# Second FFN of a decoder step: which engine forms the sums of weights and their low parts

## The reference

```python
def swiglu(x, w_gate, w_up, w_down):
    return (jax.nn.silu(x @ w_gate) * (x @ w_up)) @ w_down

h = h + 0.5 * swiglu(rmsnorm(h, ffn2_norm), ffn2_w_gate, ffn2_w_up, ffn2_w_down)   # D=1024, D_FF=2816
```

## Time and profile before

| | |
|---|---|
| three runs | 1963.45, 1974.09, 1972.76 us; median 1972.76 |
| the profiled execution | 1961.99 us |
| its span, first to last instruction | 1960.2 us, granted clock 0.985 |
| TensorE matmul busy | 1888.5 us, 96% |
| VectorE busy | 1115.8 us, 57% |
| ScalarE busy | 504.4 us, 26% |
| GpSimd busy | 536.9 us, 27% |

### The profile page before, as it was taken

How to read it: one execution, slowest core, us unless ns; L and a number is a source line. 1 busy time by engine, 2 the same in 40 slices (tenths; PEclk the granted TensorE clock), 3 DMA queues, 4 the chain that set the end, 5 groups by cost and what they waited for, 6 DMA issues and landing times.

```text
span 1960.2 us, 31184 instructions
## 1 busy us (share of the span) xinstructions
PE 1888.5 (96%) x12097; PEld 1865.1 (95%) x12097; DVE 1115.8 (57%) x1962; ACT 504.4 (26%) x927; POOL 536.9 (27%) x606
## 2 busy tenths in 40 slices
PE   7999999999999999999999997999999999999998
PEld 6999999999999999899999987899999999999997
DVE  6556455554545556613775588655565556455646
ACT  5331211111121112432111435322222223222223
POOL 3388200000000000401995035322332223222320
PEclk8999999999999999899999997999999999999999
DMA  4122211112121211046113610111111111111112
GB/s 149 42 65 82 64 32 44 53 32 64 32 64 32 63 33 44 22 100 113 41 44 71 150 43 28 43 55 44 54 44 55 43 55 44 55 44 55 44 47 90
DMA packets 152061, 111.56 MB, mean 57 GB/s; under 512 B 7267, under 2 KB 144035, under 8 KB 151829
## 3 DMA queue, kind: packets, MB, share of 16 engines
q1 hardware_dynamic: 151220, 106.95, 19.3%
q0 software_dynamic: 736, 3.19, 0.6%
HBM read 97.03 MB, written 13.09 MB: 56 GB/s over the span
## 4 chain that ended last, share of the span: by engine, by line
PE 47%; DVE 8%; issue 1%; ACT 1%; DVEq 0%; ACTq 0%
PE bank_pair L780 10%; PE bank_pair L782 9%; PE bank_pair L781 9%; PE bank_down L780 5%; PE bank_down L782 5%; PE bank_down L781 5%; DVE HT L1653 2%; DVE T L1930 1%; DVE HL L2050 1%; DVE HL L1644 1%; DVE HR L2018 1%; PE bank_pair L870 0%; PE bank_down L926 0%; DVE WL L1639 0%; PE bank_pair L1028 0%
## 5 line engine op out<-in xcount | busy, mean ns | idle before, releaser
L780 PE MATMUL bank_pair<-XH,WH 128*128 128x344 f32 x1440 | 466.7, 324 | 14.9 <-POOL XL L2176 5.2
L781 PE MATMUL bank_pair<-XL,WH 128*128 128x344 f32 x1440 | 462.2, 321 | 0.0
L782 PE MATMUL bank_pair<-XH,WL 128*128 128x344 f32 x1440 | 462.1, 321 | 0.0
L1655 DVE SCALAR_TENSOR_TENSOR HT<-bank_down,HT 128x344 f32<-128x344 f32 x518 | 267.0, 516 | 324.4 <-PE bank_down L782 324.2
L780 PEld LDWEIGHTS bank_pair<-XH,WH 128*128 128x128 f32 x1440 | 272.7, 189 | 21.1 <-POOL XL L2176 8.9
L781 PEld LDWEIGHTS bank_pair<-XL,WH 128*128 128x128 f32 x1440 | 272.6, 189 | 0.0
L782 PEld LDWEIGHTS bank_pair<-XH,WL 128*128 128x128 f32 x1440 | 272.6, 189 | 0.0
L2008 DVE SCALAR_TENSOR_TENSOR HT<-bank_down,HT 128x344 f32<-128x344 f32 x264 | 134.7, 514 | 217.1 <-PE bank_down L782 217.1
L780 PE MATMUL bank_pair<-XHM,U_hi 128*128 128x344 f32 x704 | 227.6, 323 | 15.1 <-DVE HR L2018 12.8
L782 PE MATMUL bank_pair<-XHM,U_lo 128*128 128x344 f32 x704 | 226.1, 321 | 0.0
L781 PE MATMUL bank_pair<-XLM,U_hi 128*128 128x344 f32 x704 | 225.8, 321 | 0.0
(11 more groups left out here) (279 smaller groups left out, 3341.4 us busy)
## 6 DMA issues: line engine op xcount, KB each, us to landing
RAW<-in_ffn_w_gate SPq DMA_DIRECT2D x22, 512.0 KB, 5.9
RAW<-in_ffn_w_up SPq DMA_DIRECT2D x22, 512.0 KB, 6.8
RAW<-in_ffn_w_down SPq DMA_DIRECT2D x22, 512.0 KB, 3.5
RAW<-in_w_in SPq DMA_DIRECT2D x16, 512.0 KB, 4.1
DQ_raw<-in_ffn_w_down SPq DMA_DIRECT2D x29, 256.0 KB, 2.9
U_raw<-in_ffn_w_gate SPq DMA_DIRECT2D x22, 256.0 KB, 2.9
AST<-in_ffn_w_gate SPq DMA_DIRECT2D x22, 256.0 KB, 3.0
AST<-in_ffn_w_up SPq DMA_DIRECT2D x22, 256.0 KB, 2.8
```

What stands on the lines that cost most here:

```text
L780: pe.matmul(out, wh, xh, start=first, stop=False)
L781: pe.matmul(out, wh, xl, start=False, stop=False)
L782: return pe.matmul(out, wl, xh, start=False, stop=last)
L1655: ins = dve.scalar_tensor_tensor(ht, tile, scale, ht, ALU.mult, ALU.add)
```

## The change

GpSimd's loop over the passes from the second on is removed; in the first pass it works as before. VectorE forms S1, S2, S3 in the branch V2a and S4 in M3, and computes the low parts of all units: S1 and A11 in M3, S3, A21, S2, A12 in M4, S4 in V2b, and A22 in the branch V1b of the next pass. In odd passes the low parts of a quarter and of the second block of h move from the branch M5 behind the three sums in V2a. The orders of TensorE, ScalarE and SP stay as they are.

```diff
-                dve.tensor_tensor(UL[k][:, :], UR[k][:, :], f(UH[k][:, :]), ALU.subtract).then_inc(unit_ready[k], 1)
+                raw = AST[k - 2] if k in (A21, A22) else UR[k]
+                dve.tensor_tensor(UL[k][:, :], raw[:, :], f(UH[k][:, :]), ALU.subtract).then_inc(unit_ready[k], 1)
...
+            def make(t, k):
+
+                dve.wait_ge(products, unit_used(t - 1, k))
+                if k == S1:
+                    dve.wait_ge(a_in[A21], 16 * (t + 1))
+                    dve.wait_ge(a_in[A22], 16 * (t + 1))
+                    ins = dve.tensor_tensor(UR[S1][:, :], AST[0][:, :], AST[1][:, :], ALU.add)
...
+                ins.then_inc(s_made, 1)
...
+                        if name == "V1b" and t > 0:
+                            unit_lo(t, A22)
                         if name == "V2a":
+                            make(t + 1, S1)
+                            make(t + 1, S2)
+                            make(t + 1, S3)
+                        if name == "M3":
+                            c12(t)
                             unit_lo(t + 1, S1)
                             unit_lo(t + 1, A11)
-                        if name == "M3":
-                            c12(t)
-                            unit_lo(t + 1, S3)
                             quarter_lo(4 * p)
+                            make(t + 1, S4)
                         if name == "M4":
                             c21(t)
+                            unit_lo(t + 1, S3)
+                            unit_lo(t + 1, A21)
                             unit_lo(t + 1, S2)
                             unit_lo(t + 1, A12)
                         if name == "V2b":
+                            unit_lo(t + 1, S4)
                             quarter_lo(4 * p + 1)
                     else:
                         if name == "V1b":
                             mul(t, "V1b", "v", (0, 0))
+                            unit_lo(t, A22)
...
-                        if name == "M5":
-                            quarter_lo(4 * p + 2)
-                            h_lo2(p, 1)
                         if name == "M7":
                             u3_c22_u4(t)
                             mul_sum(t, "C22", (1, 2))
                         if name == "V2a":
                             if more:
-                                unit_lo(t + 1, S1)
-                                unit_lo(t + 1, A11)
+                                make(t + 1, S1)
+                                make(t + 1, S2)
+                                make(t + 1, S3)
+                            quarter_lo(4 * p + 2)
+                            h_lo2(p, 1)
                             h_lo2(p, 2)
                         if name == "M3":
                             c12(t)
                             mul_sum(t, "C12", (0, 2))
                             if more:
-                                unit_lo(t + 1, S3)
+                                unit_lo(t + 1, S1)
+                                unit_lo(t + 1, A11)
+                                make(t + 1, S4)
                         if name == "M4":
                             c21(t)
                             mul_sum(t, "C21", (1, 1))
                             h_lo2(p, 3)
                             if more:
+                                unit_lo(t + 1, S3)
+                                unit_lo(t + 1, A21)
+                                unit_lo(t + 1, S2)
                                 unit_lo(t + 1, A12)
                         if name == "V2b":
                             mul(t, "V2b", "y", (1, 0))
                             h_lo2(p, 4)
                             if more:
-                                unit_lo(t + 1, S2)
+                                unit_lo(t + 1, S4)
                             h_lo2(p, 5)
...
-            for t in range(1, PASSES):
-                make(t, S1)
-                make(t, S2)
-                make(t, S3)
-                unit_lo(t, A21)
-                make(t, S4)
-                unit_lo(t, A22)
-                unit_lo(t, S4)
```

More of the change, by code:

```diff
@@ L1996, in unit_lo @@
                 dve.wait_ge(u_hi, hi_count(t, k))
-                dve.tensor_tensor(UL[k][:, :], UR[k][:, :], f(UH[k][:, :]), ALU.subtract).then_inc(unit_ready[k], 1)
+                raw = AST[k - 2] if k in (A21, A22) else UR[k]
[6 more added lines that the diff above has]
+                    ins = dve.tensor_tensor(UR[S1][:, :], AST[0][:, :], AST[1][:, :], ALU.add)
+                elif k == S2:
+                    dve.wait_ge(a_in[A11], 16 * (t + 1))
+                    dve.wait_ge(s_made, made_count(t, S1))
+                    ins = dve.tensor_tensor(UR[S2][:, :], UR[S1][:, :], UR[A11][:, :], ALU.subtract)
+                elif k == S3:
+                    ins = dve.tensor_tensor(UR[S3][:, :], UR[A11][:, :], AST[0][:, :], ALU.subtract)
+                else:
+                    dve.wait_ge(a_in[A12], 16 * (t + 1))
+                    dve.wait_ge(s_made, made_count(t, S2))
+                    ins = dve.tensor_tensor(UR[S4][:, :], UR[A12][:, :], UR[S2][:, :], ALU.subtract)
+                ins.then_inc(s_made, 1)
             def quarter_lo(n):
@@ L2403, in make @@
             def make(t, k):
-                if t > 0:
-                    pool.wait_ge(products, unit_used(t - 1, k))
                 if k == S1:
```

## The result

The changed kernel takes 1980.78 us (median of 14 runs, 1979.01 to 1991.74); the kernel before took 1966.84 us in its 14 runs. The ratio is 1.0074, 95% interval [1.0058, 1.0089]: slower by about 14 us, where 13 were forecast. The time forecast was 1983, with a range of 1967 to 1995. Runs of one kernel spread by about 10 us, like those near 1963 and near 1973 in the prediction; in a later set of before the longest had the lowest mean granted clock, 1973.9 us at 0.978, against 1964.6 at 0.986.

A forecast was written before the change was run, and what follows sets the result against it. TensorE, busy 96%, was taken to bound the kernel, so only its waits count. 11.5 us from ten odd-pass tails plus 1.5 from the first pass gave 13.0 us slower; time 1983 us, range 1967 to 1995.

The forecast's parts named there:

- What bounds: TensorE is busy 96% of the span; only its waits, about 1.6 us a period around one place, can be gained.
- First part: Odd pass: U4 is done in time, so TensorE's wait at M3, 1.5 us a period, goes.
- Second part: Odd pass's end: VectorE's longer list makes down tiles wait; TensorE loses 2.76 against 1.6, 1.15 us a period more, 11.5 in all.
- the bounds of 0.42 and 0.69: Limits for a sum of weights on VectorE, taken as 0.60: 7 us down and 4 us up in all.
- Third part: Even passes' down tiles: slack of 0.2 us at tile 22, costed at nothing.
- Fourth part: Loads on SP: A21's next load and quarters behind it come later, the first 2.9 us, covered by VectorE's 3.95 us idle.
- Fifth part: End of the first pass: V1b of the second pass waits for A12 and starts at 1242.5, 1.5 us more, once.
- The sum: 11.5 + 1.5 = 13.0 us slower; time taken as 1983.
- one more choice: Base time for before: the sum gives 1975.0 on the profiled run, 1985.8 on the median, 1981.1 on the mean; 1983 taken.
- No change: Rival: VectorE takes over only what GpSimd took from it, tail 1.15 us shorter; +2 to +9 us, chance 0.3.
- Faster: Rival: M3's wait goes and nothing replaces it, tail at most 11.8 us; -14.6 us, 1958, chance 0.07.
- GpSimd's blocking would balance what VectorE takes over: VectorE's tail: ground of the no-change rival, chance 0.3; forecast instead 1.47 us returned against 4.6 added.

The follow-up runs named there:

- experiment 5: experiment 3 with late low parts spread: A21, A22 in the next pass's V1b, S2, S1 in M1, S3, S4 in M2; first pass A21 behind A12; 1951.33 us.
- experiment 8: experiment 5 with the sums S1 to S4 taken from VectorE and given to GpSimd; 1948.74 us, ratio 0.9903 to the kernel before.
- experiment 9: experiment 1 with the low parts of S1, S3 and S2 of odd passes moved into the next pass, GpSimd as before; 1949.87 us.
- experiment 2: Changed kernel with the low parts of S3, A21, S2 and S4 of odd passes done in the next pass; 1967.64 us.
- experiment 7: Changed kernel with the low parts of A21, S4 and A22 given back to GpSimd, sums still on VectorE; 1998.98 us.
- experiment 3: experiment 2 plus S1's low part in the next pass, the fourth `HL` ahead of S4's sum, and an own order in the first pass; 1959.60 us.
- experiment 4: Changed kernel with the sums S1 to S4 given back to GpSimd, all low parts still on VectorE; 1964.82 us.
- experiment 6: Changed kernel with the fourth `HL` behind the low parts of S3 and A21 in odd passes; 1994.11 us.
- experiment 1: Kernel before with only the odd-pass quarter's and second h block's low parts moved behind those of S1 and A11; GpSimd keeps its work; 1983.28 us.
- experiment 10: Changed kernel with the fourth `HL` behind S3's low part alone in odd passes; 1980.72 us.

## Why the prediction was right

*What bounds.* TensorE's waits did decide. Their 1.6 us a period are the whole room: experiments 5, 8 and 9 took it.

*First part, M3's wait goes.* Right: no wait there, M3 started at its time with 0.07 us of restart.

*Second part, the tail.* Right in each step. From the start of the three sums, A11's low part ended after 7.65 us (7.54 forecast), the fourth `HL` after 9.66 (9.52), the addition of tile 0 after 14.37 (14.22). The losses over TensorE's pace were 0.26 at V1a, 1.00 at tile 0, 1.36 at tile 2 and 0.1 or less at each restart, together 2.9 us; forecast were 2.76. The text ahead of the prediction says that six more operations of 128x512 stand between U4 and the addition; six is the count from the three Winograd sums on, without the quarter, as the prediction uses it, and between the low part of unit 4 and the addition it is three. A sum of weights lasts 0.68 or 0.69 us on VectorE and takes 0.60 from start to start, as taken from the low parts; the bounds of 0.42 and 0.69 were not needed. Experiment 2 shows the cause: with four operations less ahead of it, the addition starts 2.2 us earlier and tile 2 no longer waits.

*Third part, the even passes.* Right: behind tile 2 no tile waits in the changed kernel. That the slack at tile 22 is thin was shown by experiment 7: two low parts longer by 0.65 us made just this tile wait 0.55.

*Fourth part, the loads.* Right for the changed kernel: VectorE still idles 3.95 us at the opening of an odd pass (the row at 1522.25). In another order of the first pass it was not free: in the second pass of experiments 3, 5 and 8 a quarter's load, late behind A21's, held M6 once, for 2.59, 1.91 and 1.09 us.

*Fifth part, the first pass.* 1.6 us for 1.5 forecast: V1b of the second pass starts at 1245.63, and this execution came to the place 3.0 us later than before's, so 1242.6 against 1242.5.

*The sum.* 13.0 us forecast; 14.3 by the profile (12.7 and 1.6) and 14 by the medians. The term that was a little small is the tail, by 0.12 us a period (1.27 for 1.15), in part from the distances behind instructions that need the result of the one before: S2 starts 0.82 us after S1, for 0.74 forecast. The time of 1983 rests on one more choice, a time for before between that of the profiled execution and the three runs' median; 1983 less 13 is 1970, and the 14 runs gave 1966.84. That this choice came within 4 us is in part luck, the 13 us are not.

*The rivals.* No change would have needed a shorter tail; the tail was longer. Faster would have needed a tail of at most 11.8 us; experiment 5 has one of 11.6 (1514.95 to 1526.59), and it is faster. That GpSimd's blocking would balance what VectorE takes over is answered in both directions: experiment 4 is 16 us faster than the changed kernel with the sums on GpSimd, experiment 7 18 us slower with low parts there. It hangs on which instruction is beside which. The Trainium skill (Perfetto Trace Analysis, section Optimizing Scalar/DVE Operations) says only that such a move might not help; these two runs show that it can help or harm. The Trainium skill's rule that the two lock each other out for a whole instruction (SBUF — State Buffer, section SBUF: two separate sides) agrees with 3.13 us for two `HL` beside 1.31 and 1.57.

*What the prediction did not see.* It priced a wait by its length. In the changed kernel that was right: its 2.6 us fall into pieces of 0.2, 1.0 and 1.4, and in the profiled execution the granted clock stayed at 1.00 behind all of them. The prediction did not ask for this, so here it had luck: in a list only a little different (experiment 6) the same standstill cost 13 us more. The same blind spot, and the blocking that moved to other instructions, spoiled the expectation of experiment 1.

## What to carry to other kernels

When TensorE waits for another engine, write down that engine's list from the last result it needs to the next thing it must deliver, at the distances of the trace, and compare it with TensorE's own time over the same stretch. Removing one wait by moving work behind it only moves the wait if the list is too long; moving work behind the *next* delivery removes it, and here that gave 13 to 15 us with no change of engine (experiment 9). Spread what is put off, since a burst of six makes a new wait, and where a wait of TensorE can't be avoided, two of 1 us were cheaper here than one of 2.

## What the runs showed of the hardware

- Two waits of TensorE that differ little in length differ much in price. Behind waits at tile 0 of 1.92 to 2.06 us idle (experiments 1 and 6) the granted clock stood at 0.50 for about 3.4 us, matmuls at 0.29 us each, in 18 of 20 periods. Behind 1.42 to 1.50 us (experiment 10) it did so in one of ten, behind two pieces of 0.9 us that lie 2 us apart (experiment 7) in two of ten. It never did behind before's 1.28, behind the 0.84 of experiment 2 or the 1.17 of experiment 4, nor behind the changed kernel's 0.84 and 1.20, ten periods each.
- Length alone does not decide. V1b of the second pass starts after the same 2.06 us idle in the changed kernel and in experiments 2 and 6; in the first no fall follows, in the other two one does. M6 of the second pass starts after 2.59 us in experiment 3 and 1.91 in experiment 5, without a fall. What else decides is open.
- A fall is cheaper where a wait for VectorE follows it: 1.5 us in experiment 1, 0.66 in experiment 10, nothing to be seen in experiment 7, where tile 2 then no longer waits.
- Of the VectorE instructions beside GpSimd's, those with both inputs in SBUF became long (0.51 to 1.60, 0.52 to 1.07); the three Winograd sums, which read PSUM, did not: 1.54 us beside GpSimd and 1.56 without it. The blocking goes by instruction and is not a share: in experiment 1 two GpSimd instructions in a row cost the two `HL` beside them 2.2 us.
